# GpSimd takes the remainder of weight piece 5 of every expert over from VectorE, in a decoder step with a mixture of experts

## The reference

```
logits = x2 @ w_router + b_router;  top_val, top_idx = top_k(logits, 4);  gates = softmax(top_val)
for each expert e, on the rows xb of its tokens:
    g = minimum(xb @ w_gate[e] + b_gate[e], 7.0)
    u = clip(xb @ w_up[e] + b_up[e], -7.0, 7.0)
    h = (u + 1) * (g * sigmoid(1.702 * g))
    out = h @ w_down[e] + b_down[e]
y[token] = sum over its 4 experts of out * gate
```

## Time and profile before

| | before |
|---|---|
| median of three runs | 1789.86 us |
| span of the profiled execution, first to last instruction | 1777.6 us |
| TensorE busy | 1603.4 us (90%) |
| VectorE busy | 1342.5 us (76%) |
| ScalarE busy | 1049.6 us (59%) |
| GpSimd busy | 150.0 us (8%) |
| mean granted TensorE clock | 0.918 of full speed |

### The profile page before, as it was taken

The page is one execution under the profiler, slowest core; times in us unless marked ns, Lnnn a source line. Parts: engine busy times, 40 slices in busy tenths (PEclk is TensorE's granted clock), DMA queues, the critical chain, the costliest instruction groups (busy, mean ns, idle before and its releaser), DMA issues.

```text
span 1777.6 us, 22637 instructions
## 1 busy us (share of the span) xinstructions
PE 1603.4 (90%) x7434; PEld 1111.2 (63%) x7434; DVE 1342.5 (76%) x1550; ACT 1049.6 (59%) x945; POOL 150.0 (8%) x157
## 2 busy tenths in 40 slices
PE   2998967889399999999999999999999999999980
PEld 2996535654266666666666666666666666666650
DVE  5310453433489889999999999898889989899987
ACT  3332123332277777777777677776767777676761
POOL 1000001000100010000010000010000000100003
PEclk9998575569699999999999999999999999999995
DMA  7523021011289999999999999999899999999956
GB/s 246 113 82 129 1 53 37 1 57 48 102 289 338 335 333 349 336 351 341 344 349 335 338 343 348 333 345 324 311 333 338 346 341 343 323 343 347 346 218 242
DMA packets 168887, 463.51 MB, mean 261 GB/s; under 512 B 14396, under 2 KB 28352, under 8 KB 168064
## 3 DMA queue, kind: packets, MB, share of 16 engines
q1 hardware_dynamic: 149664, 430.11, 68.0%
q10 hardware_dynamic: 11800, 15.96, 3.4%
q0 software_dynamic: 7392, 17.05, 2.9%
HBM read 451.50 MB, written 21.26 MB: 266 GB/s over the span
## 4 chain that ended last, share of the span: by engine, by line
PE 76%; DMA 10%; DVE 5%; issue 3%; ACT 3%; DVEq 2%; ACTq 1%; POOLq 0%; POOL 0%; SPq 0%
PE ps L1428 71%; DMA reg_a<-xhat_rows,slot_tok 8%; PE ps L1431 5%; ACT ring_r L862 1%; DVEq L1325 1%; DVE reg_z L1406 1%; DMA reg_p<-in_w_in 0%; DMA out_p_n<-reg_x 0%; DVE reg_z L1409 0%; DVE reg_b L1366 0%; DVE reg_z L1419 0%; DMA reg_x<-in_x_prompt 0%; DVE reg_w L1257 0%; DVEq L1405 0%; DMA ring<-moe_rows 0%
## 5 line engine op out<-in xcount | busy, mean ns | idle before, releaser
L1428 PE MATMUL ps<-ring_r,reg_z_r 128*96 128x512 f32 x4608 | 1109.9, 397 | 0.0
L1428 PEld LDWEIGHTS ps<-ring_r,reg_z_r 128*96 128x96 f32 x4608 | 735.4, 162 | 340.6 <-issue 39.9
L386 DVE TENSOR_TENSOR ring_r<-ring,ring_r 128x2048 fp32r<-128x2048 f32 x387 | 872.4, 2285 | 59.7 <-ACT ring_r L862 57.4
L862 ACT ACTIVATE ring_r<-ring 128x2048 fp32r<-128x2048 f32 x387 | 741.5, 1917 | 230.0 <-PE ps L1428 229.3
L542 POOL DMA_INDIRECT reg_a<-xhat_rows,slot_tok x33 | 81.6, 2474 | 505.6 <-DVE slot_dst L1327 505.6
L882 ACT ACTIVATE reg_z_r<-ps 128x384 fp32r<-128x384 f32 x130 | 59.1, 480 | 101.3 <-PE ps L1431 101.1
L1428 PE MATMUL ps<-reg_a_r,ring_r 128*128 128x260 f32 x576 | 106.5, 284 | 0.0
L1333 DVE TENSOR_TENSOR reg_z_r<-ps,reg_z_r 128x384 fp32r<-128x384 f32 x130 | 68.7, 548 | 36.1 <-ACT reg_z_r L882 36.1
L550 POOL DMA_INDIRECT moe_rows<-reg_a,slot_dst x33 | 31.5, 954 | 740.1 <-ACT reg_a L876 740.1
L1428 PEld LDWEIGHTS ps<-reg_a_r,ring_r 128*128 128x128 f32 x576 | 89.7, 188 | 1.0 <-issue 0.9
L1428 PE MATMUL ps<-ring,reg_a 128*128 128x512 f32 (+1 forms) x160 | 77.3, 642 | 1.9 <-DVE reg_a L1075 1.0
(11 more groups left out here) (285 smaller groups left out, 1198.8 us busy)
## 6 DMA issues: line engine op xcount, KB each, us to landing
ring<-in_w_gate SPq DMA_DIRECT2D x131, 1024.0 KB, 7.4
ring<-in_w_up SPq DMA_DIRECT2D x128, 1024.0 KB, 5.2
ring<-in_w_down SPq DMA_DIRECT2D x128, 1024.0 KB, 7.1
ring<-in_w_in SPq DMA_DIRECT2D x9, 1024.0 KB, 13.5
ring<-moe_rows SPq DMA_DIRECT2D x4, 2048.0 KB, 15.2
ring<-in_w_out SPq DMA_DIRECT2D x4, 1024.0 KB, 4.9
reg_x<-in_x_prompt SPq DMA_DIRECT2D x4, 512.0 KB, 4.6
reg_x<-in_x_prompt ACTq DMA_DIRECT2D x4, 512.0 KB, 4.0
```

The costliest lines, as they stand in the source:

```text
L386: return eng.tensor_tensor(rest_r(k), w, rounded_r(k).bitcast(F32), ALU.subtract)
L862: act.activation(rounded_r(k), ring[:, slot_of(k), :], ACT.Copy).then_inc(hi_ready, 1)
L1428: return pe.matmul(out, lhsT, rhs, start=start, stop=stop, skip_group_check=True)
```

## The change

GpSimd computes the remainder of piece 5 of every expert, at the head of its turn: it waits for `hi_ready` of that piece, subtracts, and counts a new semaphore `lo_pool`; the scatter and the gather follow behind it. VectorE leaves piece 5 out. TensorE waits for `lo_pool` ahead of the product of piece 5, and the other waits for `lo_ready` count 11 pieces for an expert in place of 12.

```diff
+POOL_PIECE = 5
@@ GpSimd, in the loop over pairs
                         t = [pool.snap(again * NE + pair * 2 + k) for k in range(4)]
+                        t12 = pool.snap(t[0] * N_PIECE)
                         for u in range(2):
+                            alone(pool, hi_ready, t12 + (N_PIECE * u + POOL_PIECE + 1))
+                            split(pool, N_PIECE * u + POOL_PIECE).then_inc(lo_pool, 1)
                             scatter(1 - u, t[u + 1])
                             alone(pool, ex_psum, t[u])
                             gather(1 - u, t[u + 2])
@@ VectorE
                             one_hot(1 - u, bass.ds(pair * 2 + (u + 1), 1))
-                            for n in range(3, 7):
+                            for n in (3, 4, 6):
                                 rest_of_piece(k + n, p12)
@@ TensorE
-            def product(k, bank, x, p12):
+            def product(k, bank, x, p11, t0):
 
-                pe.wait_ge(lo_ready, p12 + (k + 1))
+                if k % N_PIECE == POOL_PIECE:
+                    pe.wait_ge(lo_pool, t0 + (k // N_PIECE + 1))
+                else:
+                    pe.wait_ge(lo_ready, p11 + (lo_before(k) + 1))
```

More of the change, by code:

```diff
@@ L337, in hybrid_step @@
         hi_ready = sem("hi_ready")
-        lo_ready = sem("lo_ready")
+        lo_ready, lo_pool = sem("lo_ready"), sem("lo_pool")
         pick_ready, g_ready, sg_ready, yrow_ready = sem("pick_ready"), sem("g_ready"), sem("sg_ready"), sem("yrow_ready")
@@ L436, in _ @@
             all_used, out_0, out_1 = sp.snap(turns * N_PIECE + N_FIRST), sp.snap(turns * 8), sp.snap(turns * 8 + 16)
-            all_split = sp.snap(turns * N_PIECE + AHEAD)
+            all_split = sp.snap(turns * (N_PIECE - 1) + AHEAD)
             with sp.Fori(1, PASSES) as again:
@@ L1789, in _ @@
                         t0 = pe.snap(again * NE + pair * 2)
-                        t8, p12 = pe.snap(t0 * 8), pe.snap(t0 * N_PIECE)
+                        t8, p11 = pe.snap(t0 * 8), pe.snap(t0 * (N_PIECE - 1))
                         for u in range(2):
@@ L1796, in _ @@
                             for n in range(4):
-                                product(k + n, 0, eX, p12)
+                                product(k + n, 0, eX, p11, t0)
                             make_list(1 - u, t + 1, bass.ds(pair * 2 + (u + 1), 1))
@@ L1800, in _ @@
                             for n in range(4, 7):
-                                product(k + n, 2, eX, p12)
+                                product(k + n, 2, eX, p11, t0)
                             pe.wait_ge(g_ready, t + 1)
                             transpose_h(0, t)
-                            product(k + 7, 2, eX, p12)
+                            product(k + 7, 2, eX, p11, t0)
                             transpose_rows(1 - u, t8 + (16 if u == 0 else 32))
@@ L1808, in _ @@
                             bias_rows_of(2, 4, u)
-                            product(k + 8, 4, eH, p12)
+                            product(k + 8, 4, eH, p11, t0)
                             transpose_h(1, t)
-                            product(k + 9, 4, eH, p12)
+                            product(k + 9, 4, eH, p11, t0)
                             pe.wait_ge(hlo_ready, t * 2 + 2)
-                            product(k + 10, 4, eH, p12)
-                            product(k + 11, 4, eH, p12)
+                            product(k + 10, 4, eH, p11, t0)
+                            product(k + 11, 4, eH, p11, t0)
 _INS = ["x_prompt", "x_sample", "state_C", "state_n", "state_m", "cache_k", "cache_v", "rel_bias", "norm1", "w_in",
```

## The result

The changed kernel takes 1891.57 us (median of 4 runs, 1891.09 to 1894.04) against 1792.95 (4 runs); the ratio is 1.056, with a 95% interval of 1.053 to 1.059. It is slower by some 100 us. The profiled execution of the changed kernel took 1891.8 us for a span of 1890.0.

A forecast was written before the change was run, and what follows sets the result against it. TensorE's products were taken to bound the loop, the gather's DMA nearly as late. Period 37.87 + 2.6 wait + 1.3 clock = 41.8 us against 38.65; 32 turns give +100, span 1878, plus 12.3 makes 1890 us; range 1825 to 1965.

The forecast's parts named there:

- Removed: VectorE: 32 remainders of 2.29 us leave it, value 0, since piece 6 still waits for its hi from ScalarE.
- The subtraction: GpSimd's piece 5: 4.70 us, from 1036.26 to 1040.96, 3 us before TensorE wants it.
- The scatter's term: GpSimd's scatter behind the subtraction: starts 0.85 us after it, at 1041.8, and lands 3.9 us later, at 1045.7.
- D: Delay of `slots` on VectorE, which waits for the scatter's landing: 3.3 us later, 1045.7 in place of 1042.37.
- Wait (a): TensorE's wait for the first half of h: D less a margin of 1.8 us, giving 1.5 us.
- Wait (b): TensorE's wait for the gathered rows: D + landing - 9.12, with landing 8.4, giving 2.6 us and containing (a).
- The clock: TensorE's product after a wait of this size runs at a lower granted clock, costing 1.3 us more each turn.
- The sum: Loop period 41.8 us against 38.65, over 32 turns +100 us; profiled span 1878, plus 12.3 us around it, 1890 us.
- The port rule: VectorE's two-input and GpSimd's SBUF-reading instructions exclude each other; piece 6 stands until 1040.96, a 2.0 us floor under D.
- rival 2: Small D, at the floor of 2.0, clock kept: 1806 us; with the clock's 1.3 us, 1848 us; chance 0.13.
- the shorter gather: TensorE's wait for the rows: D under 1.8 us and a 6.4 us landing remove waits; 1765 us, chance 0.03.
- Rival 1: GpSimd loses the port race, subtraction ends up to 2.3 us later: D 5.6, period 44.1, 1964 us; chance 0.12.

The follow-up runs named there:

- wait-only run: Against the kernel before: GpSimd waits for the hi of piece 5 ahead of the scatter but computes nothing; 1795.33 us, ratio 0.9985.
- tiny subtraction: Against the kernel before: a 128 x 2 subtraction on GpSimd, after wait and drain, ahead of each scatter; 1768.42 us, run again 1773.48 us, ratio 0.989.
- scatter-first run: Against the changed kernel: GpSimd's scatter put back ahead of the subtraction; 1868.22 us, ratio 1.041 to the kernel before the change.

## Why the prediction was right, and where it was not

- **Removed: 0.** Right, and shown by the run without any remainder of piece 5 (ratio 1.002).
- **The subtraction.** Forecast from 7.8 to 12.5 us after the first product and 4.70 us long. Measured 4.60 us, ending at 12.5. TensorE never waited for piece 5.
- **The scatter's term was mis-sized.** The step "starts 0.85 us later and lands 3.9 us after its start" gave 4.75 us from the end of the subtraction. The 0.85 us did not come (0.17), but its instruction takes 2.80 us, and it lands 5.8 after its start: 5.97 us. The wait-only run and the tiny subtraction show why: beside VectorE's piece 6, which itself waits for GpSimd, the instruction ends only 0.81 us after VectorE's. I had taken the landing from scatters that ran when VectorE made one-hot rows or was idle.
- **D.** Forecast 3.3, measured 99.71 - 81.03 - 13.95 = 4.7 us, just outside the 2.5 to 4.5 that the forecast's chance was given to.
- **Wait (a), the half of h.** Forecast 1.5 us, measured 83.3 / 32 = 2.6, since D is larger; a margin of 1.8 us and 2.8 of wait make 4.6, so the margin was right.
- **Wait (b), the rows.** I had it decide; measured 5.7 us in all. The gather lands after 7.9 us where I took 8.4, and (a) now covers it. The reason given, fewer loads in flight while TensorE stands, fits with the scatter-first run, where TensorE did not stand ahead of it: 9.2 us; no run isolates it. Too small a D and too long a landing in part cancel: 2.6 us of waiting forecast, 2.9 measured (92.1 / 32), where the formula with the measured medians gives 4.7 + 7.9 - 9.12 = 3.5. The rest of the difference is in the clock: the waits for the rows, 11 in all, stand behind products that ran at full speed, and where the product behind (a) was slow, the rows were there before TensorE wanted them. In the changed kernel a turn paid for the clock or for the rows; the sum counts both in every turn.
- **The clock.** Forecast 1.3 us for each turn. The rest of the period, 42.18 - 37.87 - 2.9, is 1.4. But it isn't the same in each turn. These are two stretches of the changed kernel behind waits of 2.70 and 2.77 us, with PE, PEld, DVE, ACT, POOL, granted clock:

```profile
1062.00:1068.00 6.00, 5.35 (x24) 3.97 (x24) 5.86 (x5) 0.89 (x2) 0.00 (x0) 0.72 0.54 208
...
1105.00:1110.00 5.00, 4.20 (x24) 2.86 (x24) 5.00 (x5) 2.01 (x2) 0.00 (x0) 1.00 0.72 233
```

  Behind the first the product of 12 took 4.37 us, behind the second 2.99:

```profile
1063.20 4.37 PE L1435 MATMUL ps<-ring_r,reg_z_r 128*96 128x512 f32 x12
```

  The trace of before had both cases too: a wait of 1.57 us at 593 us with a product of 3.02 behind it, and one of 1.66 at 1249 us with 4.58. I had read the waits of 2.01 and 0.35 us alone. The sign "granted clock under 1.0 in every stretch of an expert" did not come.
- **The sum.** +100 us forecast; the profiled spans differ by 112.4, the runs by 99. That the time came within 2 us of 1890 is partly luck. I read the 12.3 us between the span of before and its median as lying around the span; 1891.8 for a span of 1890.0 shows that only 1.8 us do, and that the profiled execution of before was a quick one. Too small a sum (a period of 41.8 against 42.18) and too large a remainder cancelled.
- **The port rule.** Piece 6 takes 4.11 us and ends 2.16 us after GpSimd's subtraction (1095.67 against 1093.51), so the exclusive port of the Trainium skill, "SBUF — State Buffer", "Who interferes with whom", holds between the two subtractions, and the floor of 2.0 us under D was a good one: with the scatter out of the way D was 1.8. What I had wrong is its weight. I called it inside the sum, and it is, but by itself it keeps most of the loss: rival 2, which has D at this floor, gives 1848 us with the clock lost, and the scatter-first run took 1868.
- **Rivals.** GpSimd never lost the race (4.60 us in every turn). The small-D case and the shorter gather did not come, and the scatter's landing is waited for. Rival 1's "price 3.1 for the clock and the rest" doesn't fit its own period: 44.1 is 37.87 + 4.9 + 1.3. Of the signs of being right, the one that TensorE waits for the gather in nearly every turn failed as well: it did so in 11.

## What to carry to other kernels

Before work is given to an idle engine, list what stands behind it in that engine's queue and who waits for that; here the helper's own two transfers paced the bottleneck. List too what the helper's reads will hold up on the engine that is to be relieved: with the scatter put back first, VectorE's piece 6 still stood still for 1.8 us, and 4.1 of the 5.6% stayed. As much work, placed where neither mattered, was free. Ask too whether the relieved engine bounds anything: one that waits for another at its next instruction gives nothing back. And a wait of TensorE can cost more than its length, by an amount that differed with where it fell, so that 35 us less of waiting shortened the profiled span by only 22 us.

## What the runs showed of the hardware that was not expected

- An indirect DMA's instruction on GpSimd is 0.93 to 0.99 us long when VectorE makes one-hot rows or is idle. Otherwise it ended, in every turn of the loop, 0.8 to 0.9 us after one of VectorE's two-input instructions: 2.14 to 2.80 us long where that was the first, 4.67, 5.26, 6.88 and 7.47 us where it was the last of several in close order. That it waits for the port is inferred from these ends. What decides between the first and the last is open: the gather of the kernel before, 2.34 us, ends at 1046.08, after VectorE's piece 7 at 1045.22, although the product with the sigmoid follows at once, and with piece 6 behind `slots` the two cases alternate at the same offset.

```profile
1042.94 2.28 DVE L386 TENSOR_TENSOR ring_r<-ring,ring_r 128x2048 fp32r<-128x2048 f32 x1
```

- TensorE's busy time grew by 36.9 us beside 77.8 us of added waits, nearly all behind piece 6, and by 48.4 us beside 42.5 us of added waits behind piece 7.
- A drain of GpSimd's queue ahead of each scatter made the kernel 1.5% faster, through gathers that land 1 us sooner. Its mechanism is open.
